# A two-layer hybrid decoder with product-key experts: the first expert pass in another order, its one-hot rows made by two engines

## What is computed

```python
def peer_ffn(x, wq, sub1, sub2, u_tab, v_tab):
    q = (x @ wq).reshape(B, S, PEER_HEADS, PEER_QDIM)             # 8 heads, 256
    s1 = einsum('bshd,nd->bshn', q[..., :PEER_HALF], sub1)        # 128 keys
    s2 = einsum('bshd,nd->bshn', q[..., PEER_HALF:], sub2)
    v1, i1 = top_k(s1, 16); v2, i2 = top_k(s2, 16)
    cand = v1[..., :, None] + v2[..., None, :]                    # 256 a head
    top_s, pos = top_k(cand, 16)
    idx = take_along_axis(i1 * 128 + i2, pos);  wgt = softmax(top_s)
    act = gelu(einsum('bphkd,bpd->bphk', u_tab[idx], x))          # 128 experts a token
    return einsum('bphk,bphkd->bpd', wgt * act, v_tab[idx])
```

## Time and profile before

| | us |
|---|---|
| median of 3 runs | 5311.94 (5308.14 to 5318.05) |
| the profiled execution | 5324.88 |
| its span | 5323.0 |
| PE busy | 4657.3, 87% |
| DVE busy | 3276.5, 62% |
| POOL busy | 2724.8, 51% |
| ACT busy | 1554.2, 29% |

### The profile page before, as it was taken

How to read it: one execution, slowest core, us unless ns; L and a number is a source line. 1 busy time by engine, 2 the same in 40 slices (tenths; PEclk the granted TensorE clock), 3 DMA queues, 4 the chain that set the end, 5 groups by cost and what they waited for, 6 DMA issues and landing times.

```text
span 5323.0 us, 73470 instructions
## 1 busy us (share of the span) xinstructions
PE 4657.3 (87%) x21202; PEld 3874.2 (73%) x21202; DVE 3276.5 (62%) x5599; ACT 1554.2 (29%) x2428; POOL 2724.8 (51%) x1485
## 2 busy tenths in 40 slices
PE   6899998889888887999869999989898888779998
PEld 5666785678788876777757667756787888767776
DVE  7322124438889775888882322243479897658888
ACT  1223213213334332333322332132133343323332
POOL 5631483565445665555457224736654456655554
PEclk9976799999999998999989667999999999889999
DMA  2210121123467999999712001202235579999996
GB/s 94 72 43 20 52 95 39 59 77 109 156 186 226 266 310 291 340 337 335 267 61 79 32 28 52 94 32 70 72 113 167 180 232 282 294 298 331 338 332 247
DMA packets 463097, 892.73 MB, mean 168 GB/s; under 512 B 41376, under 2 KB 320416, under 8 KB 459808
## 3 DMA queue, kind: packets, MB, share of 16 engines
q1 hardware_dynamic: 387424, 617.22, 36.1%
q0 software_dynamic: 73728, 268.47, 14.7%
q10 hardware_dynamic: 1728, 4.89, 0.3%
HBM read 787.65 MB, written 102.76 MB: 167 GB/s over the span
## 4 chain that ended last, share of the span: by engine, by line
PE 48%; issue 19%; DVE 14%; DMA 8%; POOL 6%; ACT 3%; SPq 1%; DVEq 1%; POOLq 0%; ACTq 0%
DMA ring<-v_tab 6%; PE pair L704 6%; PE bank L704 6%; PE bank L1003 5%; PE bank L1008 4%; PE bank L998 4%; PE pair L707 3%; PE bank L707 3%; PE bank L823 3%; PE bank L838 2%; PE bank L736 2%; POOL hn L579 2%; POOL big L579 2%; PE pair L736 2%; POOL w_lo L587 2%
## 5 line engine op out<-in xcount | busy, mean ns | idle before, releaser
L946 PE MATMUL bank<-xT,w_hi 128*128 128x384 f32 x2048 | 749.7, 366 | 275.3 <-ACT gst L1251 267.6
L587 POOL TENSOR_TENSOR w_lo<-ring,w_hi 128x1024 fp32r<-128x1024 f32 x256 | 619.5, 2421 | 713.3 <-ACT w_hi L1239 712.6
L599 POOL TENSOR_TENSOR w_hi<-ring,ones 128x1024 fp32r<-128x1024 f32 x272 | 546.5, 2009 | 715.1 <-PE bank L707 331.5
L946 PE MATMUL bank<-xl_peer,w_hi 128*128 128x384 f32 x2048 | 725.2, 354 | 0.0
L602 POOL TENSOR_TENSOR w_lo<-ring,w_hi 128x1024 fp32r<-128x1024 f32 x272 | 688.7, 2532 | 21.4
L946 PEld LDWEIGHTS bank<-xT,w_hi 128*128 128x128 f32 x2048 | 416.1, 203 | 302.8 <-ACT gst L1251 183.1
L1239 ACT CAST w_hi<-ring 128x1024 fp32r<-128x1024 f32 x256 | 268.6, 1049 | 991.4 <-DVE ring L1776 959.5
L1863 DVE TENSOR_TENSOR cl<-att,ch 128x384 fp32r<-128x384 f32 x256 | 359.4, 1404 | 222.5 <-ACT ch L1298 222.3
L1245 ACT CAST w_hi<-ring 128x1024 fp32r<-128x1024 f32 x256 | 269.6, 1053 | 737.9 <-PE bank L1008 452.6
L593 POOL TENSOR_TENSOR w_lo<-ring,w_hi 128x1024 fp32r<-128x1024 f32 x128 | 306.3, 2393 | 329.9 <-ACT w_hi L1245 329.9
L998 PE MATMUL bank<-w_hi,ch 128*128 128x512 f32 x1536 | 398.1, 395 | 63.3 <-ACT ch L1298 63.3
(11 more groups left out here) (293 smaller groups left out, 8952.6 us busy)
## 6 DMA issues: line engine op xcount, KB each, us to landing
ring<-u_tab SPq DMA_DIRECT2D x1024, 128.0 KB
ring<-v_tab SPq DMA_DIRECT2D x256, 512.0 KB, 6.3
ring<-w_stream SPq DMA_DIRECT2D x240, 512.0 KB, 3.3
g_spill<-gst SPq DMA_DIRECT2D x256, 192.0 KB, 4.0
w_spill<-vg SPq DMA_DIRECT2D x12, 2048.0 KB, 8.2
w_spill<-att SPq DMA_DIRECT2D x12, 2048.0 KB, 9.5
vg<-w_spill SPq DMA_DIRECT2D x32, 768.0 KB, 11.3
qk<-g_spill SPq DMA_DIRECT2D x32, 768.0 KB, 6.6
```

The lines of the kernel that those rows point to most:

```text
L587: nc.gpsimd.tensor_tensor(w_lo[s % 2][:, :], ring[2 + s % 2][:, :], w_hi[s % 2][:, :].bitcast(F32), ALU.subtract)\
L599: nc.gpsimd.tensor_tensor(w_hi[b][:, 0:n], src, ones[:, 0:1].to_broadcast([P, n]), ALU.mult)\
L946: nc.tensor.matmul(out, w_hi[s % 2][:, c * P:(c + 1) * P], dense_parts(c)[part], start=(c == 0 and part == 0), stop=False)
```

## The change

`LEAD` goes from 4 to 6, so that the one-hots belong to chunks 24 to 119 and not 16 to 111. The choice of tile 0 spreads over 16 chunks and not 12; the sparse tile's begins at chunk 20 with 12 pieces and takes ten more chunks, tile 1 the next 20, tile 2 thirty. `ROWS` places the 128 dotted rows from chunk 38 on (32 before): 18 in 18 chunks, 40 in 32, 54 in 32, 16 in 8, where it was 8 in 16, 24 in 32, 62 in 32, 34 in 16. POOL starts the first six gathers in front of chunk 36 and not 32.

In `one_hots` DVE makes both rows with one comparison each; the weight is applied by ACT (`scale_hot`), four ACTIVATEs with a scale per partition, from a copy of the weights in SBUF (`pickw`). TensorE waits for ACT's semaphore. `iota`, with which the positions are compared in `choose`, is read from PSUM (`iota_p`). Chunks land in four places in turn and not in two: `ring[0]`, `ring[1]`, the fourth block of `hn` and `x_last`. A load waits for the transpose four chunks before, not two.

```diff
-LEAD = 4
+LEAD = 6
...
-ROWS = [0] * (4 * LEAD + 16) + shares(8, 16) + shares(24, 32) + shares(62, 32) + shares(34, 16) \
+ROWS = [0] * (4 * LEAD + 14) + shares(18, 18) + shares(40, 32) + shares(54, 32) + shares(16, 8) \
     + [0] * 4 + shares(SLOTS, NCHUNK - 4)
...
+        x_last = nc.alloc_sbuf_tensor_at("x_last", [P, D], F32, offset=vg_at + 4 * SP_T * D)
...
+        raw = [ring[0], ring[1], hn[:, SP_T, :], x_last]
...
+        pickw = vst[:, 0, 0, :]
+        iota_p = bank[7][:, 0:TOPK]
...
-                    sp.dma_start(ring[s % 2][32 * q:32 * q + 32, :].rearrange("a (e d) -> a e d", e=4),
-                                 src[:, :, 256 * q:256 * q + 256]).then_inc(u_ready[s % 2], 16)
+                    sp.dma_start(raw[s][32 * q:32 * q + 32, :].rearrange("a (e d) -> a e d", e=4),
+                                 src[:, :, 256 * q:256 * q + 256]).then_inc(u_ready[s], 16)
...
-                    sp.wait_ge(turned.sem, turned.at(L, "UE", i, s - 1))
+                    sp.wait_ge(turned.sem, turned.at(L, "UE", i, s - 3))
                     load_expert(L, i, s)
...
+                    if c == 4 * LEAD + 11:
+                        pool.wait_ge(eidx_ready.sem, eidx_ready.at(L, "T", 0, 2))
+                        for n in range(NG):
+                            gather(L, u_tab, n)
...
+                def scale_hot(k, s):
+
+                    b, at = s % 2, 16 * (k % 8) + 4 * s
+                    act.wait_ge(ones_ready.sem, ones_ready.at(L, "UW", k, s + 1))
+                    for j in range(4):
+                        ins = nc.scalar.activation(hot1[b][:, j, :], hot1[b][:, j, :], ACT.Copy,
+                                                   scale=pickw[:, at + j:at + j + 1])
+                    ins.then_inc(hot_ready.sem, 1)
+
+                def round_of(i, last=False, k=None, tile=DENSE):
+
+                    for s in range(4):
+                        if k is not None:
+                            scale_hot(k, s)
                         if s < 2:
                             expert_high(i, s + 2)
...
                         gelu_of(i, s)
-                        weights(s)
+                        if k is not None:
+                            weights_out(k, s)
...
-                                                   iota_f[:, :].unsqueeze(1).to_broadcast([P, HS, TOPK]), ALU.is_equal))
+                                                   iota_p.unsqueeze(1).to_broadcast([P, HS, TOPK]), ALU.is_equal))
...
+                early = 12
+                pieces = [shares(upto, 4 * LEAD - 8) + [0, 1], [0] * (4 * LEAD - 6) + shares(early, 4)]
                 for n in range(2, 4 * LEAD):
-                    advance(first, pieces[n - 2])
+                    for choice, steps in zip((first, second), pieces):
+                        advance(choice, sum(steps[n - 2:n - 1]))
                     turn(n)
...
-                    V.tensor_tensor(hot2[b], pickT[:, 1, at:at + 4].unsqueeze(2).to_broadcast([P, 4, N_KEYS]),
-                                    iota_k[:, :].unsqueeze(1).to_broadcast([P, 4, N_KEYS]), ALU.is_equal)
-                    for j in range(4):
-                        ins = V.scalar_tensor_tensor(
-                            out=hot1[b][:, j, :], in0=iota_k[:, :], scalar=pickT[:, 0, at + j:at + j + 1],
-                            in1=pickT[:, 2, at + j:at + j + 1].to_broadcast([P, N_KEYS]), op0=ALU.is_equal, op1=ALU.mult)
-                    ins.then_inc(hot_ready.sem, 1)
+                    if k % 8 == 0 and s == 0:
+                        V.tensor_copy(pickw, pickT[:, 2, :])
+                    for z in range(2):
+                        ins = V.tensor_tensor(hot[b][:, z, :, :], pickT[:, z, at:at + 4].unsqueeze(2).to_broadcast([P, 4, N_KEYS]),
+                                              iota_k[:, :].unsqueeze(1).to_broadcast([P, 4, N_KEYS]), ALU.is_equal)
+                    ins.then_inc(ones_ready.sem, 1)
...
-                pieces = [shares(upto, 16), [0] * 16 + shares(upto, 14) + [0, 1], [0] * 32 + shares(upto, 30) + [0, 1]]
+                pieces = [shares(upto - early, 10), [0] * 10 + shares(upto, 20) + [0, 1], [0] * 32 + shares(upto, 30) + [0, 1]]
```

More of the change, by code:

```diff
@@ L286, in build @@
         win = [a[:, at:at + 4 * ND].rearrange("p (b i t) -> p b i t", b=NB, t=WB) for a in wst_at for at in (0, 2048)]
-        hot = qk[:, :, :].rearrange("p (z b) n -> p z b n", z=2)
-        hot2 = [hot[:, 0, b, :].rearrange("p (t n) -> p t n", n=N_KEYS) for b in range(2)]
-        hot1 = [hot[:, 1, b, :].rearrange("p (t n) -> p t n", n=N_KEYS) for b in range(2)]
+        hot = [qk[:, 2 * b:2 * b + 2, :].rearrange("p z (t n) -> p z t n", n=N_KEYS) for b in range(2)]
+        hot1, hot2 = ([hot[b][:, z, :, :] for b in range(2)] for z in range(2))
         pickT = bank[6][:, 0:3 * P].rearrange("p (a k) -> p a k", a=3)
+        pickw = vst[:, 0, 0, :]
+        iota_p = bank[7][:, 0:TOPK]
         gst = [gst_all[:, n * ND:(n + 1) * ND] for n in range(4)]
@@ L324, in build @@
         wq_ready = [sem(f"wq_ready{s}") for s in range(4)]
-        u_ready = [sem(f"u_ready{z}") for z in range(2)]
+        u_ready = [sem(f"u_ready{s}") for s in range(4)]
         out_done = sem("out_done")
@@ L387, in build @@
         eidx_ready = Count(sem("eidx_ready"), dict(T=(1, 2)))
+        ones_ready = Count(sem("ones_ready"), dict(UW=(WROUNDS, 4)))
         hot_ready = Count(sem("hot_ready"), dict(UW=(WROUNDS, 4)))
@@ L485, in _ @@
                     load_expert(L, 0, s)
-                for s in range(2, 4):
-                    sp.wait_ge(turned.sem, turned.at(L, "UE", 0, s - 1))
-                    load_expert(L, 0, s)
+                load_expert(L, 0, 2)
+                sp.wait_ge(proj_done, slots_done(L, "UE", 0, 0))
+                load_expert(L, 0, 3)
                 with sp.Fori(1, LEAD + 1) as i:
@@ L512, in _ @@
                 for s in range(2):
-                    sp.wait_ge(turned.sem, turned.at(L, "UE", ROUNDS["UE"] - 1, s + 3))
+                    sp.wait_ge(turned.sem, turned.at(L, "UE", ROUNDS["UE"] - 1, s + 1))
                     load_value(L, 0, s)
@@ L653, in _ @@
                 split_rounds(L, "WQ")
-                with pool.Fori(0, LEAD + 4) as r:
+                with pool.Fori(0, LEAD + 2) as r:
                     for c in range(4):
                         expert_low(L, r, c)
[L658 to L662, removed]
+                n, used = 0, 0
+                for c in range(4 * (LEAD + 2), 2 * NCHUNK):
                     if c < NCHUNK:
@@ L1277, in _ @@
                     expert_high(0, s)
-                with act.Fori(0, LEAD - 1) as i:
+                with act.Fori(0, LEAD - 2) as i:
                     round_of(i)
                 soft(0, wts)
+                round_of(LEAD - 2)
                 round_of(LEAD - 1, tile=0)
@@ L1287, in _ @@
                             soft(d + 2, wts)
-                        round_of(LEAD + 8 * d + y, weights=lambda s: weights_out(8 * d + y, s),
-                                 tile=DENSE if y < 7 else d + 1)
+                        round_of(LEAD + 8 * d + y, k=8 * d + y, tile=DENSE if y < 7 else d + 1)
                 with act.Fori(LEAD + WROUNDS, ROUNDS["UE"] - 1) as i:
@@ L1782, in _ @@
                     dve.wait_ge(drained_sem[s], drnd(L, "UE", 0) + 1)
+                V.tensor_copy(iota_p, iota_f[:, :]).then_inc(hn_ready.sem, 1)
                 V.scalar_tensor_tensor(out=pair[:, :], in0=x[:, SP_T, :], scalar=stat[:, 3, SP_T:SP_T + 1], in1=nwb[:, :],
@@ L1785, in _ @@
                 turn(1)
+                dve.wait_ge(hn_ready.sem, hn_ready.at(L, "N2", 0, TT + 2))
+                stand(dve)
+                upto = KEYS_PIECES + BEFORE_SOFT
                 first = chain(best_keys(last_keys, LAST, 0, 1), choose(0, wts))
-                pieces = shares(KEYS_PIECES + BEFORE_SOFT, 4 * LEAD - 4) + [0, 1]
+                sparse_choice = choose(SP_T, wts_s)
+                second = chain(best_keys(last_keys, LAST, SP_T, SP_T + 1), sparse_choice)
+                early = 12
+                pieces = [shares(upto, 4 * LEAD - 8) + [0, 1], [0] * (4 * LEAD - 6) + shares(early, 4)]
                 for n in range(2, 4 * LEAD):
-                    advance(first, pieces[n - 2])
+                    for choice, steps in zip((first, second), pieces):
+                        advance(choice, sum(steps[n - 2:n - 1]))
                     turn(n)
@@ L1826, in _ @@
                 used = 0
-                sparse_choice = choose(SP_T, wts_s)
-                upto = KEYS_PIECES + BEFORE_SOFT
-                pieces = [shares(upto, 16), [0] * 16 + shares(upto, 14) + [0, 1], [0] * 32 + shares(upto, 30) + [0, 1]]
-                choices = [chain(best_keys(last_keys, LAST, SP_T, SP_T + 1), sparse_choice),
+                pieces = [shares(upto - early, 10), [0] * 10 + shares(upto, 20) + [0, 1], [0] * 32 + shares(upto, 30) + [0, 1]]
+                choices = [second,
```

10 lines of the change are left out of this document (5 added, 5 removed).

## The result

The changed kernel takes 5160.13 us (median of 4 runs, 5156.43 to 5166.62); the kernel before, run beside it, 5310.73 us. The ratio is 0.9716, 95% interval 0.9699 to 0.9732: 2.8% faster, some 150 us. The forecast was 5212 us, 100 less, in a range of 5150 to 5285. The profiled execution took 5166.62 us with a span of 5164.6.

A forecast was written before the change was run, and what follows sets the result against it. DVE bounds the first 80 chunks of each layer's first pass, bytes the last 48. Stretches sum to 745 us, plus 15 and 8: 768 a layer, 50 less; twice that off 5324.88, less 13, gives 5212 us, range 5150 to 5285.

The forecast's parts named there:

- chunks 0 to 23: Start of a layer's first pass: 24 transposes, 47 pieces at 1.5 us and four TensorE chunks, 115 us in sum.
- 88 to the end: Last 40 chunks of the pass: set by bytes, 73.5 MB at 296 GB/s, 248 us a layer.
- 3% on the first four: DVE-bound chunks 0 to 87, 497 us: 15 us added because the same arithmetic gave 191 where 198.0 were measured.
- ACT's loop: Two-chunk loop through transpose, cast, scaling and one-hot product: 5.1 us a chunk; 8 us a layer taken, between 0 and 29.
- The limit of the first 80 chunks, DVE: First pass before the change: the first 80 chunks are priced by DVE, the last 48 by bytes.
- In a stretch at 0.98 a shortened wait comes back as another, so I count it at nothing beside the bytes: Four landing places, last 40 chunks: shorter waits for table rows gain nothing; a higher rate would give 24 us a layer.
- all covers hold: Rival, chance 0.19: no ACT loop loss (8), DVE first at shared pair (10), faster landing (12): 30 more a layer, 5152.
- the slow rival: Rival, chance 0.08: ACT's order becomes the bound, 7.1 us a chunk on 96 chunks, 29 us a layer slower, 5370.
- I am wrong if TensorE or its weight load waits mostly for the ACT scaling: Sign in the profile after: TensorE's waits falling mostly on ACT's scaling would show the forecast wrong.
- The margin is 0.14 us either way, so I take nothing: Two-input pieces at the pair DVE shares with POOL: DVE could start at 1425.52 against POOL's 1425.66; no gain counted.
- its 10 us a layer: Iota in PSUM: position comparisons stop waiting for POOL, 0.8 us for each of 12, 10 us a layer.
- DMA takes the place of DVE: Rival, chance 0.21: chunks 56 to 87 near DMA saturation, last 40 stay at 6.58 us each, 23 more a layer, 5258.

The follow-up runs named there:

- early scaling: The changed kernel with ACT's scaling of chunk s+1 moved in front of the cast of chunk s+2, except at a tile's first chunk: 5138.15 us, ratio 0.9657.
- whole stores: The changed kernel as it stands, each 2 MB store of weights issued in one piece: 5160.13 us, ratio 0.9716.
- cut stores: The changed kernel with each 2 MB weight store cut into four, one behind each of the next four loads, and SP's loop written out: 5126.61 us, ratio 0.9638.

## Why the prediction was right, and where its steps were off

| a layer, us | forecast | measured |
|---|---|---|
| chunks 0 to 23 | 115 | 103.1 |
| 24 to 37 | 84 | 85.5 |
| 38 to 55 | 108 | 113.5 |
| 56 to 87 | 190 | 197.2 |
| 88 to the end | 248 | 242.3 |
| 3% on the first four, ACT's loop | 15 + 8 | in the above |
| sum | 768 | 741.6 |

- The way and the size were right, 150 us against 100. The limit of the first 80 chunks, DVE, was the right one: 2.34 us for transpose and one-hots, 1.17 for the pair, and for the three DVE stretches together 396 us against 382, 4% over where 3% had been added. Most of what they are over is ACT's loop: with the early scaling the three take 382.8.
- Chunks 0 to 23 were priced 12 us too dear. A piece here is not 1.5 us: DVE is busy 88.7 us, of which 24 transposes at 1.24 take 30, so that 47 pieces have at most 59, 1.25 each. The view of chunks 0 to 23 has TensorE busy 99.6 of 103.1 us: it, not DVE, sets them.
- "In a stretch at 0.98 a shortened wait comes back as another, so I count it at nothing beside the bytes": this step failed. The places give 59 us alone and 63 in company, 30 a layer. 296 GB/s was taken for what the engines can move; it was a mean over hold-ups, of which the 10.30 us wait of the earlier trace rows is one. Like bytes ran at 311, 318 and 336 GB/s in other runs. The rival "all covers hold" at 5152 had this in it, with 12 us a layer, and came closest to the time, by luck in part: it took ACT's loop at nothing.
- The order was counted at 42 us a layer, in the expectation for it alone, and gives 22 alone and 18 in company. The misses cancelled: the order's shortfall is most of the landing places' gain. That the last stretch of the sum is right (248 against 242) is luck and no merit: without the places it takes some 24 us more.
- The one-hots, 25 us a layer forecast for them alone, give 21 alone and 18 in company.
- ACT's loop was put at 8 us a layer between 0 and 29. The early scaling takes back 13 and 8 in chunks 24 to 87 of the two layers with whole stores, 16 and 19 with cut ones. Its mechanism was right and the size too small; the slow rival had the right place and the wrong price. The forecast had said "I am wrong if TensorE or its weight load waits mostly for the ACT scaling". That sign came: 70.5 us, against 11 for GELU in the same pass. It was a poor sign, since TensorE had waited longer for GELU before (267.6 us in both layers).
- "The margin is 0.14 us either way, so I take nothing": something was there. The two-input product fell from 2247 to 1700 ns, because fewer of them begin in POOL's subtraction: 16 times 0.55 or 9 us a layer, near the 10 that "all covers hold" had for it.
- Iota was worth its 10 us a layer only in the kernel before; beside the others nothing that shows.
- "DMA takes the place of DVE", 5258 us, did not come: chunks 56 to 87 ran at 265 GB/s and 0.87.

Left open: what part of the cut stores' gain the loop's turn has (cut stores with the loop kept, or the loop written out with whole stores, would tell), how the remaining 31 us of four places with cut stores come about, and why one of five runs with iota alone was 19 us slower than the others.

## What to carry to other kernels

A stretch at a DMA share of 0.98 is not proof that bytes bound it: look at where the waits fall. If they come once in so many chunks, look on the issuing queue at what stands in front of that load, a large transfer or a loop's turn, and try to cut or move it before adding buffers. Look at every such place and not at the longest alone: here the longest gap came only where the loop turned.
An edit that is to test one cause should leave the loop around it as it is.
Work moved to an idle engine costs by its place in that engine's order, not by its duration: here 1.26 us of scaling behind a cast that waits cost 8 to 19 us of a layer more than in front of it.
Parts of a change are worth other amounts alone than together (alone they sum to 170 us, the whole gives 150), so a sum can be right with its terms wrong.

## What the hardware showed

- Behind a store of 2 MB the next transfer left 0.8 us later and four transfers took 4.3 to 4.6 us to issue in eleven cases of fourteen, against 1.86 ordinarily. Where SP's loop jumped back behind such a store the next left only after 5.4 to 8.3 us, ten times of ten. Behind a 512 KB store, with the loop written out, it left after 0.7 us.
- The same pass moved its last 40 chunks at 311 GB/s with whole stores and at 336 with cut ones.
- A comparison of 128x1024 took 2034 ns beside GpSimd with both inputs in SBUF and 1215 with one in PSUM; the two-input product behind it took 2308 and not 2247.
- The two-input product took 1.21 us, and 2.6 to 3.0 us in the mean when it began while GpSimd's subtraction ran, so that what it costs in all hangs on when DVE arrives: 1700 ns in the mean in the kernel after, 2546 in the same kernel without the new one-hots.
